# Refilling a double-buffered expert weight tile in four parts as TensorE finishes with each, instead of whole after the expert's last projection

## What is computed

```python
def expert_block(args):
    xe, e = args
    gu = xe @ w_gate_up[e] + b_gate_up[e]        # first projection, 1024 -> 2048
    gt, up = jnp.split(gu, 2, axis=-1)
    ...
    act = (up + 1.0) * (gt * jax.nn.sigmoid(SWIGLU_ALPHA * gt))
    return act @ w_down[e] + b_down[e]           # second projection, 1024 -> 1024
```

## Time and profile before

| what | value |
|---|---|
| median of 3 runs | 1682.44 us (1682.2 to 1687.22) |
| span of the profiled execution | 1684.8 us |
| the profiled execution's own time | not given apart from its span |
| TensorE matmuls, busy | 1441.6 us (86%) |
| weight loads of TensorE, busy | 670.7 us (40%) |
| VectorE, ScalarE, busy | 489.9 us (29%), 216.7 us (13%) |
| data moved by DMA | 446.92 MB, of it 435.88 MB on queue q1, SyncE's |
| instruction packets (q8) | 154, 2.52 MB |
| mean granted TensorE clock | 0.921 |

### The profile page before, as it was taken

One profiled execution on the slowest core, in us unless ns is written; L12 is line 12 of the kernel. 1 busy time (PEld: TensorE's weight loads), 2 busy tenths in 40 slices (PEclk: granted clock), 3 DMA queues, 4 the chain that ended last, 5 costly groups with the idle time before them and its releaser, 6 DMA issues.

```text
span 1684.8 us, 17303 instructions
## 1 busy us (share of the span) xinstructions
PE 1441.6 (86%) x6338; PEld 670.7 (40%) x6339; DVE 489.9 (29%) x1237; ACT 216.7 (13%) x364; POOL 36.5 (2%) x44
## 2 busy tenths in 40 slices
PE   6997999989797977979788979779797887979786
PEld 4674677964332322323222323223232332323222
DVE  1694644335521311212131213212121221213123
ACT  2111432101101111011111011110111101011102
POOL 3120010000000000000000000000000000000000
PEclk9998998879698989989898989999898988989899
DMA  9657210133849798797918897987979779797921
GB/s 248 136 94 98 100 50 1 51 115 151 319 164 417 316 392 331 306 416 310 406 54 362 329 416 305 372 346 314 414 290 416 305 321 400 307 417 311 366 93 53
DMA packets 83060, 446.92 MB, mean 265 GB/s; under 512 B 6225, under 2 KB 7137, under 8 KB 50001
## 3 DMA queue, kind: packets, MB, share of 16 engines
q1 hardware_dynamic: 79600, 435.88, 67.0%
q0 software_dynamic: 2720, 7.13, 1.8%
q10 hardware_dynamic: 576, 1.31, 0.3%
HBM read 439.92 MB, written 4.39 MB: 264 GB/s over the span
## 4 chain that ended last, share of the span: by engine, by line
PE 83%; issue 9%; DMA 4%; DVE 2%; ACT 2%; ACTq 0%; DVEq 0%; SPq 0%
PE ps L1008 27%; PE ps L1019 15%; PE ps L665 8%; PE ps L982 6%; PE ps L1026 6%; PE ps L1003 5%; DMA arena<-in_w_main 2%; PE ps L883 2%; DMA arena<-in_b_gate_up 1%; PE ps L876 1%; PE ps L770 1%; PE ps L704 1%; PE ps L990 1%; PE ps L649 1%; PE ps L1084 1%
## 5 line engine op out<-in xcount | busy, mean ns | idle before, releaser
L1008 PE MATMUL ps<-arena 128*64 128x512 f32 (+1 forms) x2176 | 480.0, 602 | 0.0
L1008 PEld LDWEIGHTS ps<-arena 128*64 128x64 f32 (+1 forms) x2176 | 174.4, 139 | 303.2 <-issue 303.2
L1019 PE MATMUL ps<-arena 128*64 128x512 f32 (+1 forms) x1088 | 258.7, 608 | 19.1 <-ACT arena L605 17.5
L1491 DVE TENSOR_SCALAR arena<-ps 128x512 f32<-128x512 f32 (+1 forms) x34 | 23.5, 693 | 849.4 <-PE ps L1008 849.4
L1003 PE MATMUL ps<-arena 128*64 128x512 f32 (+1 forms) x272 | 105.3, 842 | 139.3 <-issue 138.2
L665 PE MATMUL ps<-arena 128*128 128x320 f32 x576 | 160.9, 442 | 18.9 <-DMA arena<-in_w_main 13.3
L1019 PEld LDWEIGHTS ps<-arena 128*64 128x64 f32 (+1 forms) x1088 | 85.1, 138 | 166.9 <-issue 165.1
L665 PEld LDWEIGHTS ps<-arena 128*128 128x128 f32 x576 | 111.7, 195 | 67.7 <-issue 23.6
L982 PE MATMUL ps<-arena 128*64 128x512 f32 (+3 forms) x420 | 114.3, 609 | 8.7 <-DMA arena<-in_b_gate_up 4.8
L1026 PE MATMUL ps<-arena 128*128 128x512 f32 (+3 forms) x228 | 101.9, 605 | 3.8 <-ACT arena L588 1.4
L598 ACT ACTIVATE arena<-arena 128x512 f32<-128x512 f32 x32 | 20.2, 632 | 658.3 <-DVE arena L1491 658.3
(11 more groups left out here) (280 smaller groups left out, 1008.0 us busy)
## 6 DMA issues: line engine op xcount, KB each, us to landing
arena<-in_w_gate_up SPq DMA_DIRECT2D x128, 2048.0 KB, 24.7
arena<-in_w_down SPq DMA_DIRECT2D x64, 2048.0 KB, 12.5
arena<-in_w_main SPq DMA_DIRECT2D x40, 512.0 KB, 3.6
arena<-in_w_merge_out SPq DMA_DIRECT2D x1, 3072.0 KB, 10.1
arena<-in_w_conv_out POOLq DMA_DIRECT2D x1, 2048.0 KB, 13.2
arena<-in_w_delta_out SPq DMA_DIRECT2D x1, 2048.0 KB, 8.4
out_delta_s<-arena POOLq DMA_DIRECT2D x1, 2048.0 KB, 18.8
arena<-in_xT SPq DMA_DIRECT2D x1, 1280.0 KB, 7.1
```

Of the source, the lines that this page charges most:

```text
L1008: m = pe.matmul(outs[q], tokens[:, k % 4, k // 4], w[:, k, q * 512:(q + 1) * 512], start=False, stop=(k == KD - 1))
L1019: m = pe.matmul(ps[slots * c:slots * (c + 1), 2, :], actT[:, k % 4, a:a + slots], dn[:, k, c * 512:(c + 1) * 512], start=(k == 0), stop=(k ...
```

## The change

SyncE's wait is taken apart. `late_over(e)` reads the flag and waits for late blocks if there are any, and now stands first. Then each of the four parts of gu(e+2) is issued when `up(e)` has finished its two slices of that part; for this `up` raises a semaphore, now `up_mm`, four times an expert. Only then SyncE waits for `y_mm` and issues dn(e+1). VectorE's `clamp` waits for the fourth count of its expert. A late block's `up` still raises its own semaphore once.

```diff
-            def released(e):
-
-                sp.wait_ge(sem("y_mm"), e + 1)
+            def late_over(e):
+
                 later = sp.value_load(flags[0:1, bass.ds(e * LATER, 1)], min_val=0, max_val=1)
                 with sp.If(later):
                     sp.reg_add(blocks, blocks, 1)
...
             with sp.Fori(0, E // 2 - 1) as i:
                 for p in range(2):
-                    released(2 * i + p)
+                    late_over(2 * i + p)
+                    for r in range(KD // 2):
+                        sp.wait_ge(sem("up_mm"), 8 * i + (4 * p + r + 1))
+                        load_gu(2 * i + (p + 2), p, (r,))
+                    sp.wait_ge(sem("y_mm"), 2 * i + (p + 1))
                     load_dn(2 * i + (p + 1))
-                    load_gu(2 * i + (p + 2), p)
-            released(E - 2)
+            late_over(E - 2)
+            sp.wait_ge(sem("y_mm"), E - 1)
             load_dn(E - 1)
...
                         m = pe.matmul(outs[q], tokens[:, k % 4, k // 4], w[:, k, q * 512:(q + 1) * 512],
                                       start=False, stop=(k == KD - 1))
-                m.then_inc(done, 1)
+                    if waits is not None and k % 2:
+                        m.then_inc(done, 1)
+                if waits is None:
+                    m.then_inc(done, 1)
...
-                       gu[p], [(sem(f"ld_gu{p}_{r}"), 16 * i + 16) for r in range(4)], sem("h_mm"))
+                       gu[p], [(sem(f"ld_gu{p}_{r}"), 16 * i + 16) for r in range(4)], sem("up_mm"))
...
-            def clamp(n, gate, mm, clamped, i):
-                dve.wait_ge(mm, i + 1)
+            def clamp(n, gate, mm, count, clamped):
+                dve.wait_ge(mm, count)
...
-                    clamp(P, ps[:, 0, :], sem("h_mm"), sem("clamped"), e)
+                    clamp(P, ps[:, 0, :], sem("up_mm"), 8 * i + (4 * p + 4), sem("clamped"))
```

More of the change, by code:

```diff
@@ L1514, in late_block @@
                 weigh(e, lambda t: pk[rows(t), t, LATE:2 * LATE], its)
-                clamp(2 * LATE, ps[0:2 * LATE, 0, :], sem("late_h_mm"), sem("late_clamped"), m)
+                clamp(2 * LATE, ps[0:2 * LATE, 0, :], sem("late_h_mm"), m + 1, sem("late_clamped"))
                 swiglu(2 * LATE, ps[2 * LATE:4 * LATE, 0, :], sem("late_sig"),
```

## The result

The changed kernel takes 1697.34 us (median of 5 runs, 1691.91 to 1700.06), the kernel before 1682.44: a ratio of 1.0075, interval 1.0053 to 1.0097. The forecast was 1694. In its profile the span is 1694.8 us where the earlier trace rows have 1684.8. Executions in a slower state of the core (one of 3740 us and one of 2857 us in the sets of runs 1 to 4) stand in no time or ratio given here.

What follows compares the result with a forecast made beforehand. The loop was held not short of weights; each jump's instruction fetch paid about 4.0 us for engines busy with weights. Even half +4, late expert +8, clock 0: +12 on 1682.44 gave 1694 us, range 1676 to 1716.

Steps and rivals of the forecast that it cites:

- The late expert: Rounds around expert 10's late block: its changed load order costs +8.2 us together (bounds 3 and 11).
- The wait for dn(11): In `down` of expert 11: starts 1.0 us late for its weights, then waits again for 1.7; +2.7 us.
- the second stop of 1.7: Inside `down` of expert 11, at 912.5: another wait of 1.7 us for the second half of its weights.
- The jump behind it: Jump back after expert 11: the gap that cost 5.47 us now meets busy engines, +4.0 us.
- The third piece: Round after expert 11: loads pushed back leave the even half's fetch fully contended, +1.5 us.
- The even half: End of the even `down`, idle before: loads now delay the odd `up`'s fetch 0.3 us in 14 halves, +4 us.
- rival (a): Even half fully contended: every fetch there waits, 14 x 1.5 = 21 us instead of 4; 1711 us, chance 0.12.
- The jump stays contended: Jump back at 737.62: the weight stream ends near 742, 4 us after it, so its 4.0 us are not won.
- The gap doesn't shrink with an earlier stream: At 14 jumps back: the stream starts 0 to 1.0 us earlier, the gap gets no shorter; 0 (bounds -14 and 0).
- rival (b): At 14 jumps: fetch waits for a transfer's end, so an earlier stream gives back 0.5 us each, -7; 1683, chance 0.14.
- Rival (c): Late round costs only the wait for expert 11's `down` weights, 1685 us, or the change is empty, 1682; chance 0.13.
- Rival (d): Jump's fetch suffers from how much is queued: 14 gaps fall from 9.45 to 5.5 us, -55; 1631 us, chance 0.17.

Runs made afterwards that it cites:

- runs 1 to 4: In order: changed kernel again, 1696.44 us; changed kernel with `down` weights first behind a late block, 1695.05; changed kernel without late blocks, 1631.79; kernel before without them, 1627.74.
- run 1: The changed kernel measured again with nothing altered, as yardstick: 1696.44 us, 1.0063 of the kernel before.
- run 7: The kernel before, with two of the next even expert's four first-projection parts issued only after the odd expert's `down`, ahead of all else: 1615.97 us, 0.9581.

## Why the prediction was right

*Sign and size:* +12 us forecast, +14.9 in the medians, +0.75%. The sign was right because the waits were read first: no row of the loop waited for weights, so an earlier load had nothing to give, and what it could spoil was the one gap in which the DMA engines had been out of the fetch's way. That the size came so near is in part luck, as the terms show.

*The late expert* was the main term, and near: 8.2 forecast, 9.6 and 8.3 measured, but of other pieces. The wait for dn(11) cost 3.1 us (4.2, less the 1.1 for ScalarE) against 2.7; it came in one stop ahead of `down`, and the second stop of 1.7 did not come, perhaps because the first matmuls, at 0.50, reached the second half later. The jump behind it costs 5.15 more instead of 4.0 (4.3 in run 1). The third piece, 1.5 us for the even half of the following round, did not come: no gap stands there. The other 1.3 us come from where stretches of low clock fell; a matmul group of the late block took 8.74 us instead of 7.05, for example.

*The even half* was wrong: +4 us forecast, none found. The fetch did come 2 us later, as reckoned for a contended one, but the odd `up` started at 705.39 as ever, with the packet of 704.6 to 706.6 only just moving. From the first matmul of the even `down` to the first of the odd `up` it is 6.92 us in both kernels (mean of the thirteen ordinary rounds between two gaps). The step that failed is that the odd `up` "would stand" for what of the delay isn't covered: this packet is not what it waits for. With it falls rival (a).

*The jump stays contended:* right; all fourteen gaps stayed above 9 us. The margin was reckoned wrong: 708.63 + 30.5 is 739.1, not "near 742", and so 1.5 us behind the jump, not 4. It did no harm, since the next `down` weights follow at once (99.8% from 735.0 on). (The first gap is 9.23 us; the 9.02 given for it belongs to another.) That the gaps grew by 0.15 to 0.24 us was not foreseen, 2 to 3 us in all, and no run explains it. It happens to fill the place of the even half's 4 us: the sum is better than its terms.

*The gap doesn't shrink with an earlier stream:* right. The `down` weights left 0.85 us earlier and the mean gap grew, from 9.45 to 9.69 us, which speaks against rival (b). The Trainium skill (DMA: Bandwidth & Descriptors, Queues, rings and completion order) has a DMA engine drain a whole packet of one queue before it switches to another. As the measure of this wait the trace doesn't bear that rule out, since the gap did not follow the stream.

*Rival (c)*, a late round that costs only the wait, fell with the gap of 10.62. *Rival (d)*, that the fetch suffers from how much is queued, asked for gaps below 8 us once only 4.2 MB are issued behind a `down`: after the change only the two `down` transfers are issued in the gap (735.09), and no gap fell below 9.27. In run 7 the gap shown is short although four transfers, 8.4 MB, are issued within it. What counts is whether the engines are busy when the fetch is asked for.

## What to carry to other kernels

Where a loop's program is fetched anew at each jump back, count the DMA engines as TensorE's supplier there: look at what moves at the instant of the jump, not at their mean load. Here the weights were never late, and arranging their idle time around the jump brought 4% while loading them earlier cost 0.7%. And when a load is split or moved ahead, look at the rare branch too: in SyncE's single order, what was moved ahead of a wait is ahead of the next urgent load as well.

## What was not expected

A gap with free engines is 4.6 us, under the 5.47 of the only example in the kernel before; there, the weights had stopped only just ahead of the gap (the stretch to 913 in the earlier trace rows is busy throughout), while in run 7 the 6 us from 652 on are nearly idle. The first packet started 0.9 us into that gap, in run 7 0.1 us on the mean, which is most of the difference; what held it back was not tried.

Shorter gaps gave some of their gain back. In run 7 eleven of fifteen odd `down`s took 8.6 to 8.8 us, as the one of 647.88 above, against four of fifteen in the kernel before: at 1.7 us each, some 12 us more. The one of 647.88 had a granted clock of 0.55 in its first 3.4 us, much as in the earlier trace rows. The first matmuls of a round won back 0.4 us each, so that an ordinary round is 4.5 us shorter, and its gap 4.9. What decides where the lower clock falls was not tried.
